# One 256-column value product for two heads instead of two of 128 columns, in the attention of a three-layer kernel

## The reference, cut to what matters

```python
def global_gqa(q, k, v, sink=None):                      # kind "b"
    def block(qb):                                       # 128 queries at a time
        logits = jnp.einsum('bqkgd,btkd->bkgqt', qb, k) * scale
        p = jax.nn.softmax(logits, axis=-1)
        return jnp.einsum('bkgqt,btkd->bqkgd', p, v)     # k: key head, g: its 2 query heads

def diff_attention(q, k, v, lam, ...):                   # kind "c": 4 heads, each with its own values
    p = jax.nn.softmax(logits, axis=-1)
    w = p[:, :, 0] - lam * p[:, :, 1]
    return jnp.einsum('bhqt,bthd->bqhd', w, v)

def window_gqa_latent(q, k, v, k_ctx, v_ctx, sink):      # kind "d": band of |i - j| <= 128, all context keys, a sink
    ...
```

## Time and profile before

| | us |
|---|---|
| time, median of 3 | 2341.92 |
| lowest, highest | 2341.69, 2344.62 |
| the profiled execution's own time | 2344.62 |
| its span | 2342.8 |
| PE busy in it | 2081.0 (89%) |
| DVE busy | 1153.4 (49%) |
| ACT busy | 727.5 (31%) |

### The profile page before, as it was taken

One profiled execution on the slowest core, in us unless ns is written; L12 is line 12 of the kernel. 1 busy time (PEld: TensorE's weight loads), 2 busy tenths in 40 slices (PEclk: granted clock), 3 DMA queues, 4 the chain that ended last, 5 costly groups with the idle time before them and its releaser, 6 DMA issues.

```text
span 2342.8 us, 25891 instructions
## 1 busy us (share of the span) xinstructions
PE 2081.0 (89%) x9648; PEld 1350.9 (58%) x9648; DVE 1153.4 (49%) x2688; ACT 727.5 (31%) x1612; POOL 56.7 (2%) x98
## 2 busy tenths in 40 slices
PE   5888898999789697898998859968899997999999
PEld 2644655555444364565555424535578885887887
DVE  1284183545446447155655365773744444333333
ACT  2212324544431122234554110113633223222222
POOL 2000000000000000000000200000000000000000
PEclk9999999999899798999999979987899997999999
DMA  8111111010451211111000512112033331333331
GB/s 262 37 33 40 32 37 37 1 37 28 153 216 63 50 47 36 30 52 37 16 22 10 173 37 64 56 33 55 10 90 93 103 95 52 99 99 92 97 99 63
DMA packets 149148, 157.25 MB, mean 67 GB/s; under 512 B 5724, under 2 KB 110336, under 8 KB 149024
## 3 DMA queue, kind: packets, MB, share of 16 engines
q1 hardware_dynamic: 142592, 135.81, 19.1%
q0 software_dynamic: 6432, 19.78, 3.0%
HBM read 151.37 MB, written 4.19 MB: 66 GB/s over the span
## 4 chain that ended last, share of the span: by engine, by line
PE 73%; DVE 17%; ACT 5%; issue 3%; DMA 2%; POOL 1%; DVEq 0%; ACTq 0%; POOLq 0%
PE psum L697 15%; PE psum L1104 9%; PE psum L1105 9%; PE psum L1106 9%; PE psum L709 5%; PE psum L872 5%; PE psum L724 5%; PE psum L1002 4%; PE psum L905 3%; PE psum L886 3%; PE psum L660 2%; DVE stats L1848 2%; ACT arena L1368 1%; PE psum L742 1%; ACT arena L1201 1%
## 5 line engine op out<-in xcount | busy, mean ns | idle before, releaser
L697 PE MATMUL psum<-arena 128*128 128x512 f32 (+2 forms) x1536 | 557.9, 520 | 8.7 <-ACT arena L1201 4.6
L1201 ACT ACTIVATE arena<-psum 128x256 f32<-128x256 f32 (+6 forms) x524 | 205.9, 421 | 764.5 <-PE psum L660 240.6
L697 PEld LDWEIGHTS psum<-arena 128*128 128x128 f32 x1536 | 293.2, 198 | 235.9 <-issue 208.1
L1104 PE MATMUL psum<-part,part 128*128 128x512 f32 x896 | 350.9, 392 | 10.8 <-DVE part L2179 8.8
L1105 PE MATMUL psum<-part,part 128*128 128x512 f32 x896 | 350.2, 391 | 0.0
L1106 PE MATMUL psum<-part,part 128*128 128x512 f32 x896 | 350.0, 391 | 0.0
L2175 DVE TENSOR_TENSOR part<-arena,part 128x1024 fp32r<-128x1024 f32 x112 | 137.3, 1226 | 251.5 <-ACT part L1201 251.5
L1848 DVE TENSOR_REDUCE stats<-psum 128x1 f32<-128x768 f32 (+6 forms) x208 | 138.7, 708 | 159.0 <-PE psum L872 157.6
L1201 ACT ACTIVATE part<-arena 128x1024 fp32r<-128x1024 f32 (+1 forms) x176 | 151.4, 895 | 200.4 <-PE psum L1106 140.9
L1104 PEld LDWEIGHTS psum<-part,part 128*128 128x128 f32 x896 | 169.3, 189 | 47.4 <-issue 12.2
L1106 PEld LDWEIGHTS psum<-part,part 128*128 128x128 f32 x896 | 169.2, 189 | 35.6
(11 more groups left out here) (253 smaller groups left out, 1943.4 us busy)
## 6 DMA issues: line engine op xcount, KB each, us to landing
arena<-in_w_in SPq DMA_DIRECT2D x72, 512.0 KB, 4.5
arena<-in_w_mlp SPq DMA_DIRECT2D x64, 512.0 KB, 4.0
arena<-in_w_ada SPq DMA_DIRECT2D x48, 512.0 KB, 5.8
arena<-in_w_gate SPq DMA_DIRECT2D x32, 512.0 KB, 4.1
arena<-in_w_out SPq DMA_DIRECT2D x24, 512.0 KB, 3.7
arena<-in_w_in SPq DMA_DIRECT2D x20, 256.0 KB, 3.0
arena<-in_w_branch SPq DMA_DIRECT2D x8, 512.0 KB, 4.5
arena<-in_x POOLq DMA_DIRECT2D x4, 512.0 KB, 9.0
```

The lines of the kernel that those rows point to most:

```text
L697: mm = pe.matmul(bank(b)[:, c0:c1], lhs[:, k, m * P:(m + 1) * P], ring.view(tag, l, k // 2)[:, k % 2, c0:c1], start=k == 0, stop=k == kt - 1)
L1104: pe.matmul(dst, lo, x_hi_, start=first, stop=False)
L1201: return act.activation(dst, src, ACT.Copy)
```

## The change

For the kinds b and d and for all of layer 2, `sum_values` does nothing for a step with e = 0. At e = 1 it sums both steps of the tile: for each block of keys it issues one matmul for heads 0 and 1 together (the two heads' transposed weights side by side, 128 + 128 columns) and one for heads 2 and 3. Kind c is as before. So that four heads can stay until then, the ring of transposed weights has 8 heads instead of 4; to make room, `prob` has 3 steps instead of 4 in layers 0 and 1, with the wait in front of the exponentials moved from step k - 4 to k - 3, and two small buffers move to another region.

```diff
-        prob = R_WORK.cut(4, 2, TOK)
-        prob_t = R_WORK.cut(4, TOK)
-        queries_t, heads_t = R_WORK.cut(2, 256), R_WORK.cut(2, 256)
+        prob = R_WORK.cut(3, 2, TOK)
+        prob_t = R_WORK.cut(8, TOK)
+        queries_t, heads_t = R_V.cut_at(0, 2, 256), R_V.cut(2, 256)
...
-            return (prob_t_2 if l == 2 else prob_t)[:, (head_number(l, k) + i) % 4, :]
+            return (prob_t_2 if l == 2 else prob_t)[:, (head_number(l, k) + i) % 8, :]
+
+        def heads_turned(l, k, i):
+
+            n = head_number(l, k - 1) % 8
+            return (prob_t_2 if l == 2 else prob_t)[:, n:n + 4, :].rearrange("p (g i) n -> p g i n", g=2)[:, :, i, :]
...
-            n = head_number(l, k) + i - 4
+            n = head_number(l, k) + i - 8
...
-            kind, m, e = steps_[k]
-            return k + 1 if kind == "c" and e % 2 == 0 else k
+            return k + 1 if steps_[k][2] % 2 == 0 else k
...
-            return (prob_2 if l == 2 else prob)[:, k % 4]
+            return prob_2[:, k % 4] if l == 2 else prob[:, k % 3]
...
             kind, m, e = attention_steps(l)[k]
-            if kind != "c":
-                return [(k, i, h) for i, h in enumerate(heads_of(kind, e))]
-            return [(k - 1, 0, e - 1), (k, 0, e)] if e % 2 else []
+            if e % 2 == 0:
+                return []
+            if kind == "c":
+                return [(k - 1, 0, e - 1), (k, 0, e)]
+            return [(k + g - 1, i, 2 * i + g) for g in range(2) for i in range(2)]
...
-                b, u = sum_bank(l, k), e // 2 if kind == "c" else e
-                if u == 0:
+                b = sum_bank(l, k)
+                if kind != "c" or e == 1:
                     open_bank(b)
...
-                    for j, (k_, i, h) in enumerate(heads):
-                        mm = pe.matmul(bank(b)[64 * j:64 * j + 64, u * P:(u + 1) * P], value(kind, s, h), head_turned(l, k_, i)[0:w, x * P:(x + 1) * P],
-                                       start=x == 0, stop=x == len(blocks) - 1)
+                    cols = slice(x * P, (x + 1) * P)
+                    for j in range(2):
+                        if kind == "c":
+                            out_, rest, pass_ = bank(b)[64 * j:64 * j + 64, (e // 2) * P:(e // 2 + 1) * P], value(kind, s, heads[j][2]), head_turned(l, heads[j][0], 0)[0:w, cols]
+                        else:
+                            out_, rest, pass_ = bank(b)[64 * j:64 * j + 64, 0:256], value(kind, s, 2 * j), heads_turned(l, k, j)[0:w, :, cols]
+                        mm = pe.matmul(out_, rest, pass_, start=x == 0, stop=x == len(blocks) - 1)
...
-                if k >= 4:
-                    act.wait_ge(*att_mm.at("t", l, k - 4, *turns_of(l, k - 4)[-1]))
+                before = k - (4 if l == 2 else 3)
+                if before >= 0:
+                    act.wait_ge(*att_mm.at("t", l, before, *turns_of(l, before)[-1]))
```

More of the change, by code:

```diff
@@ L344, in build @@
         w2 = [R_WORK.cut(HD) for _ in range(2)]
+        prob_t_at = R_WORK.start + R_WORK.at
         blocks_c = [R_WORK.cut(16, 2 * N_CMP) for _ in range(2)]
@@ L351, in build @@
         prob_2 = base[:, R_WORK.start + LT * D:R_WORK.start + LT * D + 8 * SEQ].rearrange("p (k j n) -> p k j n", k=4, j=2)
-        prob_t_2 = R_WORK.cut(4, SEQ)
+        prob_t_2 = base[:, prob_t_at:prob_t_at + 8 * SEQ].rearrange("p (k n) -> p k n", k=8)
         queries_t_2, heads_t_2 = R_WORK.cut(2, 256), R_WORK.cut(2, 256)
```

## The result

| | before | after |
|---|---|---|
| median, us | 2343.27 (4 runs, 2341.69 to 2345.12) | 2369.78 (4 runs, 2367.92 to 2372.14) |
| ratio | | 1.0113, interval 1.0096 to 1.0131 |
| profiled execution's own time | 2344.62 | 2367.96 |
| its span | 2342.8 | 2365.9 |

The change costs 26.5 us; 8 were forecast, with 2357 as the upper end. Slower was the likeliest sign, but the size was three times too small.

What follows compares the result with a forecast made beforehand. PE was taken as the bound, busy 89% of the span. Terms -2.9 - 1.4 + 9.0 + 2.05 + 2.0 - 0.6 - 0.3 + 0.5 = +8.4, taken as +8: median 2341.92 becomes 2350, range 2339 to 2357.

Steps and rivals of the forecast that it cites:

- the term for the clock: Kind d: PE idling in bare rounds (no sum) may lower the clock, 0 to +7 us, taken as +0.5.
- together -0.3: Layer 2: ten short calls -1.2 us, last tile +0.9; together -0.3, bounds -2 and +2.
- forecast by places: Attention stages: cost of longer or missing sums by what stands beside them in each round, without the clock term.
- Bare and full rounds of kind b: Six bare rounds (no sum) save 0.49 us each, -2.9; a seventh -1.4; seven full (double sum) add 1.29 each, +9.0.
- layer 0's seventh bare round: Kind b, layer 0, 256 columns of scores: without its sum, heads follows DVE's earlier second copy, -1.4 us.
- A pair side by side, whatever its width: Sum records for both PSUM halves run together, costing only their columns; rival not side by side: up to +49 us, 0.02.
- The rings: Three steps of `prob` and eight heads of `prob_t`: ACT's wait on k - 3 always over, cost 0.
- Kind d: Waits for t1's copy cover most bare and full rounds, 0; last tiles cost layer 1 +2.05, layer 0 +2.0 us.
- The clock: Rival: the clock falls in kind d's bare rounds, five lower stretches, +7 us, 2357; chance 0.11.
- longer pauses than 2 us stand in kind d already: Kind d: argument against the falling-clock rival, with most stretches there at clock 1.0.
- ten short calls: Layer 2, first 31 us at the lower clock: ten calls of short sums go, 0.12 us each, -1.2.
- Instruction Overhead: All joined sums: about 60 cycles per matmul, 464 records less give 11.6 us, 2330; under the faster rival, 0.09.

Runs made afterwards that it cites:

- rings only: Kernel before with the change's longer and shorter rings and moved buffers, every sum as before; 1.0001 against before.
- before with the delay: Kernel before plus one spare group of 24 value-product records (1.3 us) in layer 0's kind c; 0.9999 against before.
- shift: Kernel before plus two spare groups of 24 records (2.6 us) in kind b of each of layers 0 and 1; 1.0011 against before.
- joined in layer 2: Sums joined as in the change for layer 2 alone, other sums as before; 1.0023 against before, +6.4 us.
- its delayed kernel: The changed kernel plus one spare group of 24 records (1.3 us) in layer 0's kind c; 1.0098 against before.
- narrow: The changed kernel with each 256-column product issued as two of 128 columns; 1.0111 against before.
- with the copies ahead: Outside kind c, ACT copies t0 and t1 ahead of its exponentials, DVE t2 and t3; on before 2322.08 us (0.9905), on the change 2342.75 (0.9992).
- filled in d alone: The changed kernel plus unread value products of the old sums' size in kind d's bare rounds (no sum); 1.0079 against before.
- filled: The changed kernel plus unread value products of the old sums' size in bare rounds of kind d and layer 2; 2358.04 us, 1.0057 against before.
- the delays: Spare groups of 24 records in layer 0's kind c: on before 0.9999, the change 1.0098, sums joined in kind b alone 1.0054 (one), 1.0055 (two).

## Why the prediction was wrong

The step that failed is the term for the clock, "I take +0.5, since most of kind d is limited by DVE", and with it layer 2's "together -0.3". Kind d and layer 2 ran at the lower clock for longer, and in layer 2 the emptied rounds gave nothing back. To size them, the old order's kernels (before, rings only, before with the delay, shift, and for layers 0 and 1 joined in layer 2) are averaged, less their delays, and so are the three with the change's order (after, its delayed kernel, narrow):

| attention | old order | change's order | difference | forecast by places | time at the lower level, old and change's |
|---|---|---|---|---|---|
| layer 0 | 293.2 | 298.7 | +5.5 | +3.7 | 15.7, 23.9 |
| layer 1 | 203.8 | 213.2 | +9.4 | +4.4 | 8.2, 19.4 |
| layer 2 | 72.6 | 78.3 | +5.7 | -0.3 | 31.3, 38.2 |

That is 20.6 where 7.8 was forecast. The last column adds up the stretches in which the trace has the granted clock at 0.50: 26.3 us more in all. At half speed they can cost half of that, 13.1 us, and 12.8 are missing from the forecast. The remaining 5.9 of the 26.5 stand in no stage: all others together are 1.2 us longer between the same traces (1773.5 and 1774.7), and the two profiled executions of before and after are 23.3 us apart, not 26.5. I can't put them to a cause.

- *Bare and full rounds of kind b* (-2.9 - 1.4 + 9.0): right, 0.48 and 1.28 for 0.49 and 1.29; layer 0's seventh bare round gives back 1.13 (from 6.40 to 5.27) for 1.4. DVE's copy of t1 bounds the bare round: with the copies ahead it is 0.46 shorter.
- *A pair side by side, whatever its width*: right. Narrow and the change are equal within their intervals.
- *The rings*: right, 1.0001, and after the change ACT's exponentials never wait for TensorE's turns.
- *Kind d*: "A bare round waits longer for the same copy": t3 waits 1.65, and from the scores to heads are 6.62 us after (1252.62 to 1259.24) as before (1243.72 to 1250.34). So the 0 was right for the round. But the longer wait is not free: filling it, with work that nobody needs, made the kernel 5.7 us faster (filled in d alone; the intervals of the two ratios just touch). Time that TensorE idles at no cost in its round was followed by rounds at half the clock, in which its work cost double.
- *The clock*: the right mechanism was among the rivals at 0.11. In layers 0 and 1 the stages are 6.8 us above the places (14.9 and 8.1), the rival's upper end of +7 and not +0.5. Against it I had held that "longer pauses than 2 us stand in kind d already"; the trace of before has none, its longest there is 1.69. Nor do the bare rounds idle for 2.3 us in one piece: it is 0.47 and 1.65, with t2 between. What the rival's 2357 lacked is layer 2, whose first part the clock lengthens too, and the 5.9 above. It also had the clock fall only by the bare rounds of kind d, while it falls in kind d when only kind b is changed.
- *Layer 2*: two errors of about 3 us, 6.0 together. The first part was already at the lower level for its 31 us, and I had left it at that; there a joined sum's extra columns cost double, the level lasts for 34.7 us, and it comes back once for 3.4. The second is in the places. The queries' transposes wait for DVE's and ACT's copies, which the short sums hid, as in kind b. TensorE, third tile, after:

```profile
1677.79 0.92 PE L879 MATMUL psum<-arena 64*128 64x384 f32 x4
1678.64 0.87 PE L893 MATMUL psum<-ident,arena 128*128 128x128 f32 x6
1679.76 0.44 PE L667 MATMUL psum<-ident,arena 128*128 128x128 f32 x2 [0.25 <-ACT arena L1212]
1680.89 0.44 PE L856 MATMUL psum<-ident,arena 128*128 128x128 f32 x2 [0.69 <-DVE arena L1874]
1681.26 0.41 PE L879 MATMUL psum<-arena 64*128 64x31 f32 x4
...
1682.40 1.52 PE L917 MATMUL psum<-arena 128*64 128x256 f32 x12
1683.85 0.41 PE L879 MATMUL psum<-arena 64*128 64x31 f32 x4
```

and before:

```profile
1658.91 0.92 PE L872 MATMUL psum<-arena 64*128 64x384 f32 x4
1659.76 0.87 PE L886 MATMUL psum<-ident,arena 128*128 128x128 f32 x6
1660.56 0.88 PE L905 MATMUL psum<-arena 128*64 128x128 f32 x12
...
1662.01 0.44 PE L849 MATMUL psum<-ident,arena 128*128 128x128 f32 x2 [0.20 <-DVE arena L1862]
1662.38 0.41 PE L872 MATMUL psum<-arena 64*128 64x31 f32 x4
...
1664.33 0.41 PE L872 MATMUL psum<-arena 64*128 64x31 f32 x4
```

The bare round takes 3.47 us as it did with its sum; the full one 2.59 instead of 1.95. I had counted ten short calls as won, and the columns of the joined ones as given back by the bare rounds.

The rival of the Trainium skill's "Instruction Overhead" (TensorEngine Tiling (Array Packing)) is settled by narrow: 464 records more cost nothing that the runs can tell, and its estimated 11.6 us, 0.005 in the ratio, would show. The page on the clock (the Trainium skill, TensorE: Matmul & The Clock Gate, The HAM clock gate) has the lower level as the default, released by activity, and the chip's watch over activity as running freely, not reset when a kernel starts. The first agrees with filled, where work without use brought the clock back; the second may fit the stages that scatter between kernels with equal work (layer 1's end, 68.5 to 72.3), which no run here shows, and the delays show that the change's own loss in layers 1 and 2 doesn't hang on it.

## What to carry to other kernels

Before work is moved away from one place on TensorE to another, look at what its going leaves there. A pause that costs nothing in its round can be followed by rounds at half the clock, so read the granted clock by stretch and price a term for it from the stage's own lower stretches, above all where the stage already shows less than 1.00. A stage at the lower level pays double for each added column (20 records took 2.40 us for 1.31). And a sum that hides another engine's late copy is a sign to move the copy: that gave 22 us here.

## What the runs showed of the hardware

- Work that nobody reads, added to the emptied rounds, made the kernel 11.7 us faster, with the granted clock at 0.947 to 0.949 instead of 0.938 to 0.941.
- TensorE was busy for 29.66 of 31 us in layer 2's first part of the kernel before, and the granted clock stayed at 0.50; 20.11 of 21 us in the filled kernel went with 0.84.
- Pauses equal to 0.01 us (1.16 and 1.69) left the clock at its full level in one kernel and not in another.
- A stage of equal work differs by 4.4 us between two traces (layer 0's attention, 291.8 in before and 296.2 in rings only), while the medians of the two kernels are within 0.01%.
